# Quarter rows turned on VectorE and scaled on GpSimd in the expert stage, with a new order of the experts

## The reference

```python
p_g, grp = lax.top_k(p_group, 1)                       # one of 4 groups
p_e, local = lax.top_k(softmax(logits_in), 2)          # two of its 8 experts
expert = grp * 8 + local                               # 2048 (token, expert) picks
gate = p_g * p_e / sum(p_e)
# for each expert: rows of h that picked it
y = (silu(xb @ w_gate[e]) * (xb @ w_up[e])) @ w_down[e]  # 1024 -> 512 -> 1024
out = layer_norm(alpha * x + g2 * sum over the two picks of gate * y)
```

## Time and profile before

| | us |
|---|---|
| median of 3 runs | 1696.85 (1696.8 to 1698.94) |
| the profiled execution's own time | 1698.64 |
| its span from first to last instruction | 1696.9 |
| PE busy over the span | 1510.6 (89%) |
| DVE busy | 928.8 (55%) |
| ACT busy | 693.8 (41%) |
| POOL busy | 210.3 (12%) |
| first block's first product | at 1171.64 |
| last block's last product | at about 1632.7 |
| first instruction of `combine` | at 1643.12 |

### The profile page before, as it was taken

One profiled execution on the slowest core, in us unless ns is written; L12 is line 12 of the kernel. 1 busy time (PEld: TensorE's weight loads), 2 busy tenths in 40 slices (PEclk: granted clock), 3 DMA queues, 4 the chain that ended last, 5 costly groups with the idle time before them and its releaser, 6 DMA issues. The chain is left out here.

```text
span 1696.9 us, 47262 instructions
## 1 busy us (share of the span) xinstructions
PE 1510.6 (89%) x19436; PEld 1107.6 (65%) x19436; DVE 928.8 (55%) x1855; ACT 693.8 (41%) x1585; POOL 210.3 (12%) x274
## 2 busy tenths in 40 slices
PE   5799998999978899986999989965999999999868
PEld 3578886779867888874666668853555555555433
DVE  6798762332114556658899858865151553445416
ACT  5444431012234455534677745522131432444321
POOL 0000001000034445314000000000000000000024
PEclk9799999999987999997999989976999999999889
DMA  9312324542133344213011034418848779999976
GB/s 367 112 63 94 102 75 168 199 147 76 52 115 105 109 120 136 84 57 117 20 44 51 7 115 169 156 53 332 315 180 345 287 303 421 391 413 416 385 252 245
DMA packets 115268, 305.34 MB, mean 180 GB/s; under 512 B 11010, under 2 KB 57682, under 8 KB 106074
## 3 DMA queue, kind: packets, MB, share of 16 engines
q1 hardware_dynamic: 93178, 244.95, 38.3%
q0 software_dynamic: 10336, 46.67, 7.8%
q10 hardware_dynamic: 11520, 10.49, 2.0%
HBM read 256.41 MB, written 45.67 MB: 178 GB/s over the span
## 5 line engine op out<-in xcount | busy, mean ns | idle before, releaser
L2753 PE MATMUL psum<-now_hidden,i_xm 128*32 128x256 f32 x4992 | 292.0, 386 | 9.8 <-DVE now_hidden L2855 7.1
L2753 PEld LDWEIGHTS psum<-now_hidden,i_xm 128*32 128x32 f32 x4992 | 160.2, 111 | 132.9 <-issue 27.9
L2765 PE MATMUL psum<-now_down,i_hT 128*32 128x256 f32 x2464 | 147.7, 379 | 6.4 <-ACT now_down L2816 6.4
L2871 DVE TENSOR_TENSOR i_h<-i_silu,psum 128x128 f32<-128x128 f32 x78 | 22.4, 287 | 220.3 <-ACT i_silu L2809 220.3
L2799 ACT ACTIVATE i_xm<-psum,run_mod 128x128 f32<-128x128 f32 x163 | 63.4, 458 | 154.4 <-issue 128.2
L2765 PEld LDWEIGHTS psum<-now_down,i_hT 128*32 128x32 f32 x2464 | 81.3, 110 | 59.7 <-ACT now_down L2816 9.8
L2855 DVE COPY now_hidden<-raw_hidden 128x1024 f32 x168 | 104.4, 696 | 23.1 <-DMA raw_hidden<-in_w_up 14.2
L124 PE MATMUL psum<-hT_head,wm_head 128*128 128x512 f32 (+1 forms) x256 | 96.8, 378 | 11.2 <-DVE hT_rest L415 6.9
L1918 PE MATMUL psum<-dkT,f_qT 64*128 64x512 f32 (+1 forms) x384 | 90.1, 577 | 16.9 <-ACT f_E L1968 14.5
L1968 ACT ACTIVATE f_E<-psum,f_mx 128x1280 f32<-128x1280 f32 (+2 forms) x96 | 92.9, 972 | 19.2 <-DVE f_mx L2029 18.3
L124 PE MATMUL psum<-hT_rest,wm_head 128*128 128x512 f32 (+1 forms) x256 | 95.0, 371 | 0.0
(11 more groups left out here) (378 smaller groups left out, 3040.0 us busy)
## 6 DMA issues: line engine op xcount, KB each, us to landing
raw_hidden<-in_w_gate SPq DMA_DIRECT2D x22, 2048.0 KB, 26.0
raw_hidden<-in_w_up SPq DMA_DIRECT2D x22, 2048.0 KB, 31.0
raw_down<-in_w_down SPq DMA_DIRECT2D x22, 2048.0 KB, 19.9
wa_late<-in_w_ada POOLq DMA_DIRECT2D x16, 1024.0 KB, 6.1
yb<-i_y ACTq DMA_DIRECT2D x80, 128.0 KB, 10.9
wa<-in_w_ada SPq DMA_DIRECT2D x8, 1024.0 KB, 13.9
wt<-in_w_in SPq DMA_DIRECT2D x4, 2048.0 KB, 9.1
wm<-in_w_in SPq DMA_DIRECT2D x12, 512.0 KB, 3.9
```

The costliest lines, as they stand in the source:

```text
L2753: last = nc.tensor.matmul(by_blocks(hidden_bank(s)[j * SUB:(j + 1) * SUB, :]), xm[u][:, k, s * SUB:(s + 1) * SUB], columns_of(now["hidden" ...
L2765: last = nc.tensor.matmul(down_bank(s)[j * SUB:(j + 1) * SUB, :], hT[s % 2][:, k * SUB:(k + 1) * SUB], now["down"][:, k, j * WIDE:(j + 1) ...
```

## The change

1. `xg` holds the rows of one block in quarters: partition 32a+t has quarter a of row t (256 columns). POOL gathers 128 pieces of 1 KB per block, from a ring of four buffers (`RING`). `tok` therefore holds 4*token+a, and its product on PE becomes 64 products of 32-column weights with 96 columns in plain float32.
2. DVE transposes such a tile in one instruction of 128x256 (`turn_x`), four blocks ahead (`AHEAD`), at the end of each step. PE's transposes go.
3. POOL scales and shifts the transposed tile in two `tensor_tensor` instructions of 128x256 with broadcast operands (`modulate`). ACT's `shape` goes.
4. PE and ACT read one place per block, PE between the two halves of `hidden`.
5. The order: with 22 experts in use, the sorted experts are dealt in columns of ranks 0, 6, 12, 18; 1, 7, 13, 19; 2, 8, 14, 20; 3, 9, 15, 21; 4, 10, 16; 5, 11, 17.

```diff
+AHEAD = 4
+RING = SUBS
+STRIDE = 6
+def quarters(ap):
+    return ap.rearrange("t (a n) -> (t a) n", a=SUBS)
...
-        link(ts(some_long[:, :], nblk[:, :], LONG - 0.5, None, ALU.is_gt))
...
-        link(ts(by_two[:, :], by_two[:, :], -1.0, None, ALU.add))
+        nearest(whole[:, :], used[:, :], 1.0 / STRIDE, 0.5 / STRIDE - 0.5)
+        link(stt(left[:, :], whole[:, :], -float(STRIDE), used[:, :], ALU.mult, ALU.add))
...
-        ts(short[:, :], nth, -1.5, by_three[:, :], ALU.mult, ALU.add)
...
-        link(ts(pos[:, :], pos[:, :], -EXACT, None, ALU.add))
+        nearest(row_of[:, :], nth, 1.0 / STRIDE, 0.5 / STRIDE - 0.5)
+        link(stt(column_of[:, :], row_of[:, :], -float(STRIDE), nth, ALU.mult, ALU.add))
+        link(stt(pos[:, :], column_of[:, :], left[:, :], row_of[:, :], ALU.min, ALU.add))
+        link(stt(pos[:, :], column_of[:, :], whole[:, :], pos[:, :], ALU.mult, ALU.add))
...
-            last = nc.tensor.matmul(m.bank(2, QUADS), row_hot[:, n, :], part_hot[:, n, :], start=(n == 0), stop=(n == PICKS - 1))
+            for a in range(SUBS):
+                last = nc.tensor.matmul(m.bank(2, BLOCKS)[a * SUB:(a + 1) * SUB, :], row_hot[:, n, :], part_hot[:, n, :], start=(n == 0), stop=(n == PICKS - 1),
+                                        tile_position=(0, a * SUB))
...
     @block.gpsimd
     def _(pool):
-        def gather(q, i, u):
-            pool.wait_ge(x_turned[u], i)
-            pool.indirect_dma_start(out=xg[u][:, :], out_offset=None, in_=d["xn2"],
-                                    in_offset=bass.IndirectOffsetOnAxis(ap=tok[:, q:q + 1], axis=0)).then_inc(gathered[u], 16)
+        def gather(b):
+            pool.wait_ge(x_turned, b - RING + 1)
+            pool.indirect_dma_start(out=xg[b % RING][:, :], out_offset=None, in_=quarters(d["xn2"]),
+                                    in_offset=bass.IndirectOffsetOnAxis(ap=tok[:, b:b + 1], axis=0)).then_inc(gathered[b % RING], 16)
+        def each_row(w):
+            return run_mod[:, w, :].unsqueeze(2).to_broadcast([P, KD, SUB])
+        def modulate(b):
+            pool.wait_ge(x_turned, b + 1)
+            nc.gpsimd.tensor_tensor(xt[b % 2][:, :, :], xt[b % 2][:, :, :], each_row(1), ALU.mult).then_inc(x_scaled, 1)
+            if b >= RING:
+                pool.wait_ge(used["hidden"], (b - RING + 1) * KD)
+            pool.wait_ge(x_scaled, b + 1)
+            nc.gpsimd.tensor_tensor(xm[b % RING][:, :, :], xt[b % 2][:, :, :], each_row(0), ALU.add).then_inc(x_kept, 1)
+        def body(q, i, u, s):
+            b = q * SUBS + s + AHEAD
+            modulate(b)
+            gather(b + RING)
...
     @block.tensor
-        def turn_x(i, u):
-            pe.wait_ge(gathered[u], 16 * i + 16)
-            pe.wait_ge(x_kept[1 - u], i + u)
-            for k in range(KD):
-                last = nc.tensor.transpose(m.bank(k // 4)[:, k % 4 * P:(k % 4 + 1) * P], run_columns(xg[u], k), ident)
-            last.then_inc(x_turned[u], 1)
...
-            here, after = place_of(pe, b), place_of(pe, b + 1)
+            if q > LOW and s == 0:
+                ahead[:] = [place_of(pe, b), place_of(pe, b + 1)]
+            here, after = ahead
...
+            pe.wait_ge(x_kept, b + 2)
             pe.wait_ge(mixed, b)
-            hidden(b + 1, v, r, after, range(KD // 2))
-            hidden(b + 1, v, r, after, range(KD // 2, KD))
+            hidden(b + 1, r, after, range(KD // 2))
+            ahead[:] = [after, place_of(pe, b + 2)]
+            hidden(b + 1, r, after, range(KD // 2, KD))
             down(b, s, here)
...
     @block.scalar
-        def shape(i, u, ks):
...
     @block.vector
+        def turn_x(b):
+            dve.wait_ge(gathered[b % RING], 16 * (b // RING) + 16)
+            if b >= 2:
+                dve.wait_ge(x_kept, b - 1)
+            nc.vector.transpose(xt[b % 2][:, :, :], run_columns(xg[b % RING])).then_inc(x_turned, 1)
...
             mix(b + 1, (s + 1) % SUBS)
             keep_y(b, i, u, s)
+            turn_x(b + AHEAD)
...
         nc.vector.tensor_scalar(run_mod[:, 1, :], run_mod[:, 1, :], 1.0, None, ALU.add).then_inc(mod_ready, 1)
+        turn_x(0)
         for first in range(1, SLOTS):
```

More of the change, by code:

```diff
@@ L43 @@
 COUNT = 96
+QUARTER = 70
+AHEAD = 4
+RING = SUBS
 SMALL = COUNT + P
@@ L2434, in _ @@
         pool.wait_ge(token_ready, 1)
-        for u in range(2):
-            pool.indirect_dma_start(out=xg[u][:, :], out_offset=None, in_=d["xn2"],
+        for u in range(RING):
+            pool.indirect_dma_start(out=xg[u][:, :], out_offset=None, in_=quarters(d["xn2"]),
                                     in_offset=bass.IndirectOffsetOnAxis(ap=tok[:, u:u + 1], axis=0)).then_inc(gathered[u], 16)
@@ L2729, in _, with hidden @@
     def _(pool):
-        def gather(q, i, u):
-            pool.wait_ge(x_turned[u], i)
-            pool.indirect_dma_start(out=xg[u][:, :], out_offset=None, in_=d["xn2"],
-                                    in_offset=bass.IndirectOffsetOnAxis(ap=tok[:, q:q + 1], axis=0)).then_inc(gathered[u], 16)
+        def gather(b):
[15 more added lines that the diff above has]
+            gather(b + RING)
         pool.wait_ge(routed, 1)
+        pool.wait_ge(mod_ready, 1)
+        for b in range(AHEAD):
+            modulate(b)
+            gather(b + RING)
         nc.gpsimd.memset(nothing[:, :], 0.0).then_inc(nothing_ready, 1)
-        blocks(pool, start=lambda q, i, u: gather(q + 2, i + 1, u))
+        nb = blocks(pool, block=body)
+        for u in range(RING):
+            pool.wait_ge(gathered[u], ((nb + AHEAD + 2 * RING - 1 - u) >> 2) * 16)
     @block.tensor
     def _(pe):
-        def turn_x(i, u):
-            pe.wait_ge(gathered[u], 16 * i + 16)
-            pe.wait_ge(x_kept[1 - u], i + u)
-            for k in range(KD):
-                last = nc.tensor.transpose(m.bank(k // 4)[:, k % 4 * P:(k % 4 + 1) * P], run_columns(xg[u], k), ident)
-            last.then_inc(x_turned[u], 1)
-        def hidden(b, u, s, place, ks):
+        def hidden(b, s, place, ks):
             pe.wait_ge(copied["hidden"], place * KD + ks[-1] + 1)
@@ L2771, in body @@
             b = q * SUBS + s
[L2772 to L2775 removed]
+            if q > LOW and s == 0:
+                ahead[:] = [place_of(pe, b), place_of(pe, b + 1)]
+            here, after = ahead
+            r = (s + 1) % SUBS
+            pe.wait_ge(x_kept, b + 2)
             pe.wait_ge(mixed, b)
[L2777 to L2778 removed]
+            hidden(b + 1, r, after, range(KD // 2))
+            ahead[:] = [after, place_of(pe, b + 2)]
+            hidden(b + 1, r, after, range(KD // 2, KD))
             down(b, s, here)
         pe.wait_ge(routed, 1)
[L2782 removed]
         first = place_of(pe, 0)
+        ahead = [first, place_of(pe, 1)]
+        pe.wait_ge(x_kept, 1)
         for k in range(KD):
[L2785 to L2790 removed]
+            hidden(0, 0, first, range(k, k + 1))
+        blocks(pe, block=body)
     @block.scalar
     def _(act):
[L2794 to L2804 removed]
         def gate(b, s):
@@ L2819, in body @@
             b = q * SUBS + s
-            here, after = place_of(act, b), place_of(act, b + 1)
-            if X_PARTS[s][0] < X_PARTS[s][1]:
-                shape(i + u, 1 - u, X_PARTS[s])
+            if q > LOW and s == 0:
+                ahead[:] = [place_of(act, b), place_of(act, b + 1)]
+            here, after = ahead
             gate(b + 1, (s + 1) % SUBS)
@@ L2825, in body @@
                 copy_down(here + 1, b)
+            ahead[:] = [after, place_of(act, b + 2)]
             if q >= LOW or s == SUBS - 1:
@@ L2840, in _ @@
         gate(0, 0)
+        ahead = [place_of(act, 0), place_of(act, 1)]
         nq = (blocks(act, block=body, end=store) + (SUBS - 1)) >> 2
@@ L2899, in _ @@
         ahead = [after, look(2)]
+        turn_x(1)
         mix(0, 0)
+        for b in range(2, AHEAD):
+            turn_x(b)
         blocks(dve, block=body)
```

83 lines of the change are left out of this document (26 added, 57 removed).

## The result

The kernel after runs in 1687.98 us against 1696.8 us, medians of seven runs each: ratio 0.9949, interval 0.9931 to 0.9967, faster by 0.5% where next to no change was forecast. Measured again in a later series the ratio was 0.9963, 0.9945 to 0.9981, so I count it as 6 to 9 us. The profiled execution took 1691.94 us, with a span of 1689.8.

What follows compares the result with a forecast made beforehand. PE bounds the loop early, weight transfers late. Block 45 at 1426.9, down issue 1435.2, last weights 1611.5 and the tail put combine at 1644.1, 0.9 later: 1699.5 profiled, 1697.7 median, called 1698; range 1684 to 1710.

Steps and rivals of the forecast that it cites:

- the hold-up of the copies by GpSimd: DVE's bursts of weight copies: a copy waits for a whole POOL product, 1.7 us more per burst, steps of 8.1 us.
- the zeros as the tail: Stage end: SP's x1, norm rows and zeros after the last copy take 24.5 us, no longer hidden behind three blocks.
- the price of the reads: PE's block heads: without transposes and with one place read, a block goes from 5.36 to 5.33 us.
- The bounds: PE's block time: 5.0 us with no gap at all, 5.4 if a read between the halves stops PE.
- The heads close up: Rival on PE's blocks: 5.0 us each, 14.5 us back before block 45, about 1686; chance 0.08.
- Block 1: Loop start: its product at 1178.7 against 1178.33 before, bounds -1 and +8.
- The tokens: PE's token products before the first gather: 6 us, tokens 2.4 later; slow rival 11.3 us, total 1703, chance 0.15.
- Block 45: Place 9's first block in the new order: starts at 1426.9, after 44 blocks of 5.33 us plus hold-ups.
- The hold-ups: New experts' blocks before block 45: 0.5 us for single ones, 2.8 for second and third in a row, 13.7 together.
- From there to the last burst: Down issue 8.3 us after block 45's start, then ten experts in 176 us; last weights land at 1611.5.
- From the burst to the combine: Stage end: copies 6.6, SP's tail 24.5, barrier 1.5 us; combine at 1644.1, 0.9 later than before.
- the copies are not held up: Rival on DVE's bursts: rows of singles cost 1.1 us each, combine 10 us earlier, 1687; chance 0.27.

Runs made afterwards that it cites:

- reads_alone: Kernel before with only PE and ScalarE reading one place per block, PE's between the halves of the hidden product: ratio 0.9951.
- R: The reads part: one place read per block, on PE between the halves, and on ScalarE; added to the kernel before 0.9951, with the new order too 0.9986.
- X: The new x path part, off PE and ScalarE; added to the kernel before without the new reads or order, 1.0028.
- order_alone: Kernel before with only the new order of the experts: ratio 1.0062.
- reads_and_order: Kernel before with the one-place reads and the new order, x path as before: ratio 0.9986.
- x_alone: Kernel after with the old order of the experts, new x path and reads kept: ratio to before 0.9957.
- a clear end: Zeros stored early, GpSimd and transposes stopped at the last block's successor; on the kernel after 0.995, on it with the old order 0.9945.
- act_scales: Kernel after with the scaling of x moved from GpSimd to ScalarE, GpSimd keeping the gathers: ratio to before 0.9971.
- pool_ends_zeros: Kernel after with zeros stored in the first expert's blocks, and GpSimd and transposes stopping at the last block's successor: ratio to before 0.995.
- zeros_early: Kernel after with SP storing the unused quads' zeros in the first expert's blocks, not after the last weights: ratio to before 0.9947.

## Why the prediction was wrong

It forecast 1698 and 1688 was measured. The mechanisms that it named are there: the order, the hold-up of the copies by GpSimd, the zeros as the tail. The step that failed is the price of the reads: "5.36 becomes 5.33 us: the block behind the transposes had its two reads hidden behind them". The 5.33 runs to the next block's first product, so it holds the next block's reads, and the reads that I took as hidden stand ahead of it. With one read between the halves the same stretch is 5.20, the next two 5.18 and the one ahead of the transposes 5.30 (reads_alone); with the new x path, away from the bursts, all are 5.18. The bounds, 5.0 and 5.4, hold; I placed the value near the upper one, and it lies midway. "The heads close up", 0.08, at 1686, was the nearest case. That its time almost came out is in part luck: it had blocks of 5.0, and they take 5.18.

Term by term from the sort, forecast (sum's times less 1144.3), then measured in the two profiles of the kernel after:

- Block 1: +34.4; +32.9 and +31.9. The tokens were no brake: PE's products took 5.35 and 4.53 us (6 forecast), and the smaller gather, 6.5 us from issue to transpose, won more back than I gave it.
- Block 45: +282.6; +274.4 and +270.7. The blocks give 44 x 0.15 = 6.6 of the 8.2 and 11.9, the start 1.5 and 2.5. The hold-ups in all blocks, as what is left, came to 13.6 and 10.9 beside 13.7. That their sum is near is luck, for they were mis-sized in both ways: the step in a row of singles is 7.18, not 8.1 (burst 5.85, not 6.6; transpose 0.63, not 0.45), but the row has a delay at its first and last block too, 6.51 and 6.03, and in the first profile blocks 4 to 8 lost 2.4 us in small gaps on PE while the DMA was full.
- From there to the last burst: 184.6; 187.1 and 185.6. The down slot came 10.4 us behind block 45, not 8.3: ScalarE issued y stores first.
- From the burst to the combine: 32.6; 35.4 and 36.1. Two ends of equal length, one of which (GpSimd's drain) was in no term.

Sum: +499.8; +496.9 and +492.4. So the stage is 3 to 7 us shorter than forecast, and 2 to 6.5 shorter than the 498.9 of the one profile before; the medians give 6 to 9. The rest is within the spread of profiles and medians.

The rival "the copies are not held up" fell: they are, by 0.94 us a burst, 0.85 of it by the products. By the page of the Trainium skill that I had weighed (SBUF — State Buffer, Who interferes with whom) the later of two engines that want the shared port pair blocks for the whole instruction of the other. The trace fits such turns: exactly one copy for each product is longer, 1.10 or 1.11 against 0.68, and the products are longer too, 0.97 and 0.88 against 0.61, as they would be by waiting for the copy under way. It doesn't prove them. But a turn costs the burst 0.42 to 0.43, less than the 0.61 that the product takes by itself, and I had priced it at the 0.723 of another product. With the gather, which cost 0.15 in place of 0.27, that made my price too high by 0.8 us a burst, and the longest copy of the stage took 1.11, not 1.4.

Why the order is worth nothing comes out of the same counts, which I had not set side by side. The new order puts the last burst later, by 14.7 us alone, 11.9 with R (451.5 to 463.4), 5 to 10 with X and R (451.0 to 456.3 and 461.5), and leaves two blocks fewer behind it. But the combine can't come sooner than x1 and the zeros allow: from the last burst's start it is 37.6 us before, 33.1 in order_alone, 34.3 in reads_and_order. So 3 to 4.5 us come back. With the new x path GpSimd's drain makes the old order's end 42.0 long (x_alone), against 35.4, and 6.6 come back. With a clear end it is 37.6 against 29.6, and 8 come back for a last burst that is 7 later: the order is free there without the drain too.

What stays open: why two reads at the head cost 0.25 to 0.3 us a block with the new x path and 0.15 with the old one, whether their number or their place costs it, and why the full stretch of the DMA is 2 to 4 us longer with the new x path and the old order.

## What to carry to other kernels

On an engine that is busy without a gap, register reads at the head of a step are on the path: read once, behind work that has been issued already, and try that before anything larger, since here it did by itself what the whole change did. When work goes to an idle engine, ask what it shares with the engine that sets the pace, and when: the same two products cost a burst 0.85 us beside it and 0.3 or less a mix later. At the end of a stage look at when each engine reaches the barrier, with its drain: an engine that works ahead of the others finishes behind them if nothing stops it at the last item, and of two ends of equal length taking one away gives nothing.

## What the runs showed of the hardware

GpSimd's drain at the close of the stage took 7.0 us in all nine profiles with the new x path in which GpSimd works ahead of the last block, act_scales among them, where it only gathers, and 6.8 us in all four in which it stops there. With the old x path it took 10.2 to 13.3 us. It was nearly as long in pool_ends_zeros, where it ran from 1608.6 inside the loop, as in zeros_early, where it began at 1632.2 and the DMA share was 0.17 from 1630 to 1635 and 0.00 from 1635 to 1640. No run here shows what sets its length. VectorE's transpose of 128x256 by columns 8 elements apart took 0.63 us, against 0.31 for one of 128x128. 128 products of a 32-row group and 96 columns took between 4.14 and 5.35 us in the thirteen profiles that have them, after a pause of PE of 6.6 us, as against 3.59 for 16 of the full width.
